# Post-norms of a two-model transformer kernel: the last squares summed on TensorE, copies and splits moved behind

## The reference

```
def rmsnorm(x, g):
    xf = x.astype(jnp.float32)
    y = xf * lax.rsqrt(jnp.mean(xf * xf, axis=-1, keepdims=True) + RMS_EPS)
    return (y * g.astype(jnp.float32)).astype(x.dtype)

    x = x + rmsnorm(merged @ w_out[l], norm_mix_post[l])
    h = rmsnorm(x, norm_mem_pre[l])
    ...
    x = x + rmsnorm(memory_cross_attention(h, mem_n, w_mq[l], w_mkv[l], w_mo[l]), norm_mem_post[l])
    h = rmsnorm(x, norm_ffn_pre[l])
    ...
    x = x + rmsnorm(y, norm_ffn_post[l])
```

## Time and profile before

| what | value |
|---|---|
| median of three runs | 3776.49 us |
| the three runs | 3774.99, 3776.49, 3776.53 us |
| the profiled execution | 3774.35 us |
| its span | 3772.5 us |
| TensorE busy (matmuls) | 3590.9 us, 95% of the span |
| VectorE busy | 2018.5 us, 54% |
| ScalarE busy | 1441.1 us, 38% |
| DMA | 333.13 MB, mean 88 GB/s |
| mean granted clock of TensorE | 0.991 |

### The profile page before, as it was taken

One profiled execution on the slowest core, in us unless ns is written; L12 is line 12 of the kernel. 1 busy time (PEld: TensorE's weight loads), 2 busy tenths in 40 slices (PEclk: granted clock), 3 DMA queues, 4 the chain that ended last, 5 costly groups with the idle time before them and its releaser, 6 DMA issues.

```text
span 3772.5 us, 52548 instructions
## 1 busy us (share of the span) xinstructions
PE 3590.9 (95%) x19348; PEld 2948.0 (78%) x19348; DVE 2018.5 (54%) x3396; ACT 1441.1 (38%) x2252; POOL 241.9 (6%) x384
## 2 busy tenths in 40 slices
PE   8999989999999999899999988999999998899998
PEld 6788877887787887688778776788888777677886
DVE  5634466777764355677774466443233444644345
ACT  3344344332324534533233366332122234743232
POOL 0000000001000000000000052000000002620000
PEclk9999999999999999999999999999999999999999
DMA  3222322445322233144551102111211112112222
GB/s 138 89 73 95 98 81 95 144 145 195 117 95 78 73 106 112 51 143 146 187 162 56 51 2 42 45 51 61 67 61 61 56 67 56 31 45 81 97 95 83
DMA packets 113070, 333.13 MB, mean 88 GB/s; under 512 B 32792, under 2 KB 33688, under 8 KB 112408
## 3 DMA queue, kind: packets, MB, share of 16 engines
q1 hardware_dynamic: 74112, 265.23, 21.3%
q0 software_dynamic: 14400, 52.44, 4.2%
q10 hardware_dynamic: 24408, 13.46, 1.6%
HBM read 328.99 MB, written 6.00 MB: 89 GB/s over the span
## 4 chain that ended last, share of the span: by engine, by line
PE 83%; DVE 7%; ACT 5%; issue 2%; DVEq 1%; POOL 0%; DMA 0%; ACTq 0%; POOLq 0%; SPq 0%
PE PS L602 14%; PE PS L603 14%; PE PS L604 13%; PE PS L984 11%; PE PS L987 11%; PE PS L985 10%; PE PS L677 1%; PE PS L1112 1%; PE PS L771 1%; ACT PB L1671 1%; ACT FULL_P L1671 1%; PE PS L783 1%; DVE HVAL L1946 1%; DVE Y L2359 1%; DVE MX L2385 1%
## 5 line engine op out<-in xcount | busy, mean ns | idle before, releaser
L1902 DVE TENSOR_TENSOR WL<-RAW,WH 128x1024 fp32r<-128x1024 f32 x494 | 604.6, 1224 | 572.9 <-ACT WH L1330 567.4
L1330 ACT ACTIVATE WH<-RAW 128x1024 fp32r<-128x1024 f32 x494 | 521.4, 1056 | 638.6 <-PE PS L987 350.3
L602 PE MATMUL PS<-HHI,WH 128*128 128x512 f32 x1632 | 648.5, 397 | 14.7 <-DVE HLO L1939 7.5
L603 PE MATMUL PS<-HLO,WH 128*128 128x512 f32 x1632 | 642.3, 394 | 0.0
L604 PE MATMUL PS<-HHI,WL 128*128 128x512 f32 x1632 | 636.7, 390 | 0.0
L984 PE MATMUL PS<-H2HI,WH 128*128 128x512 f32 (+1 forms) x1336 | 470.8, 352 | 0.0
L985 PE MATMUL PS<-H2LO,WH 128*128 128x512 f32 (+1 forms) x1336 | 445.0, 349 | 0.0
L987 PE MATMUL PS<-H2HI,WL 128*128 128x512 f32 (+1 forms) x1336 | 388.2, 351 | 0.0
L602 PEld LDWEIGHTS PS<-HHI,WH 128*128 128x128 f32 x1632 | 306.8, 188 | 100.1 <-DVE HLO L1939 15.5
L604 PEld LDWEIGHTS PS<-HHI,WL 128*128 128x128 f32 x1632 | 306.8, 188 | 68.1
L603 PEld LDWEIGHTS PS<-HLO,WH 128*128 128x128 f32 x1632 | 307.3, 188 | 61.1 <-issue 0.5
(11 more groups left out here) (340 smaller groups left out, 5650.3 us busy)
## 6 DMA issues: line engine op xcount, KB each, us to landing
RAW<-in_stream SPq DMA_DIRECT2D x494, 512.0 KB, 3.7
MODW<-in_modw POOLq DMA_DIRECT2D x96, 512.0 KB, 4.5
bias_rows<-in_rpb ACTq DMA_DIRECT2D x8, 476.2 KB, 6.1
X<-in_x SPq DMA_DIRECT2D x4, 512.0 KB, 5.5
MEM<-in_mem ACTq DMA_DIRECT2D x2, 1024.0 KB, 4.9
CROW<-in_crow POOLq DMA_DIRECT2D x4, 512.0 KB, 4.9
BIAS<-bias_rows ACTq DMA_DIRECT2D x8, 224.0 KB, 4.7
GRID<-bias_rows ACTq DMA_DIRECT2D x8, 224.0 KB, 4.8
```

What stands on the lines that cost most here:

```text
L602: nc.tensor.matmul(out, WH[:, slot, b * P:(b + 1) * P], hi, start=start, stop=False)
L603: nc.tensor.matmul(out, WH[:, slot, b * P:(b + 1) * P], lo, start=False, stop=False)
L1330: A(WH[:, d, :], RAW[:, s, :], ACT.Copy).then_inc(high_split, 1)
L1902: TT(WL[:, d, :], RAW[:, s, :], WH[:, d, :].bitcast(F32), ALU.subtract).then_inc(split_ready, 1)
```

## The change

- `statistics(n, direct, last_square)` waits only for the adds of the first `KB - direct` squares, sums `ACC` into the bank, issues the eight dummies, waits for each of the last `direct` squares itself, and adds it into the same bank with a matmul from `SQ`. `direct` is 1, and 2 behind `w_mo`. VectorE's `add_squares` leaves those squares out.
- ScalarE squares ahead of copying, and signals the square by `sq_ready`; behind `w_mo` two squares come before two copies.
- The `split_high` of the last evacuation goes behind `root`. VectorE's matching `split_low` goes behind `residual`, except at the first model's mixer output, where it stands between `root_inverse` and `residual`.
- The table preloads at the mixer output and at `w_down` go ahead of the squares.
- Behind `w_down` TensorE waits for all `modulation` steps before `statistics`.

The diff, cut to its core (the counting of marks and the second model's parts that repeat the pattern are left out):

```diff
-            def statistics(n):
-
-                keep_clock(8)
-                m.add("sqt", KB - 1)
-                pe.wait_ge(sq_taken, m.at("sqt"))
+            def summed_over(src, n, start, stop):
+
                 for c0 in range(0, n, T):
                     c1 = min(c0 + T, n)
-                    last = nc.tensor.matmul(FLAT[:, 6 * T + c0:6 * T + c1], ONES[:], ACC[:, c0:c1], start=True, stop=True)
+                    last = nc.tensor.matmul(FLAT[:, 6 * T + c0:6 * T + c1], ONES[:], src[:, c0:c1], start=start, stop=stop,
+                                            skip_group_check=True)
+                return last
+
+            def statistics(n, direct=1, last_square=None):
+
+                m.add("sqt", KB - 1 - direct)
+                pe.wait_ge(sq_taken, m.at("sqt"))
+                summed_over(ACC, n, True, False)
+                keep_clock(8)
+                if last_square is None:
+                    m.add("sq", KB - direct)
+                for j in range(direct, 0, -1):
+                    if last_square is None:
+                        m.add("sq")
+                        pe.wait_ge(sq_ready, m.at("sq"))
+                    else:
+                        pe.wait_ge(y_squared, last_square)
+                    last = summed_over(SQ[:, (KB - j) % 2, :], n, False, j == 1)
                 last.then_inc(stat_done, 1)
...
+                pe.wait_ge(mod_used, (l + 1) * MOD_LAYER)
                 statistics(T)
...
-                A(Y[:, k, :], bank(3 * p), ACT.Copy)
-                A(dst[:, 0:n], bank(3 * p), ACT.Square, scale=D ** -0.5).then_inc(taken[p], 1)
-                split_high()
+                A(dst[:, 0:n], bank(3 * p), ACT.Square, scale=D ** -0.5).then_inc(sq_ready, 1)
+                A(Y[:, k, :], bank(3 * p), ACT.Copy).then_inc(taken[p], 1)
+                if k < KB - 1:
+                    split_high()
...
+                act.preload_act_table_set("natural_log_exp_and_others")
                 squares(of_y, T)
-                act.preload_act_table_set("natural_log_exp_and_others")
                 root(T)
+                split_high()
...
-            def add_squares(k, n, arrived):
+            def add_squares(k, n, arrived, direct=1):
 
                 if k == 0:
                     return
+                if k >= KB - direct:
+                    arrived(k)
+                    return
...
                 def post(gain, next_gain, last=False):
                     root_inverse(T)
                     residual(gain, False)
+                    split_low()
...
                 for k in range(KB):
                     add_squares(k, T, y_arrived)
-                    split_low()
+                    if k < KB - 1:
+                        split_low()
                 root_inverse(T)
...
+                split_low()
                 residual(G_MIXP, True, between=split_two)
```

More of the change, by code:

```diff
@@ L899, in _ @@
                 statistics(T)
-                m.add("sq", KB)
                 m.add("max", 16)
@@ L946, in _ @@
                     unit_out(last)
-                m.add("sq", KB // 2)
-                statistics(T)
+                statistics(T, 2)
                 sum_squares(T)
@@ L1308, in _ @@
                     quarter_down()
-                statistics(TA if full else T)
+                statistics(TA if full else T, 1, (l + 1) * KB)
         @block.scalar
@@ L1343, in square_slot, with squares @@
                 return SQ[:, k % 2, :]
-            def squares(src, n, before=None):
+            def squares(src, n, before=None, direct=1):
                 for k in range(KB):
@@ L1573, in of_mo @@
                     p = (m.n["units"] - 1) % SLOTS
-                    A(Y[:, k, :], bank(3 * p + k % 2), ACT.Copy)
-                    sq = A(dst[:, 0:n], bank(3 * p + k % 2), ACT.Square, scale=D ** -0.5)
-                    sq.then_inc(taken[p] if k % 2 else sq_ready, 1)
+                    A(dst[:, 0:n], bank(3 * p + k % 2), ACT.Square, scale=D ** -0.5).then_inc(sq_ready, 1)
                     if k % 2:
-                        split_high()
-                squares(of_mo, T)
+                        A(Y[:, k - 1, :], bank(3 * p), ACT.Copy)
+                        A(Y[:, k, :], bank(3 * p + 1), ACT.Copy).then_inc(taken[p], 1)
+                        if k < KB - 1:
+                            split_high()
+                squares(of_mo, T, direct=2)
                 root(T)
+                split_high()
                 squares_summed(of_x, T)
@@ L1609, in of_down @@
                     m.add(f"use{k % 2}")
[L1610 to L1613, removed]
+                    A(dst[:, 0:n], bank(3 * (k % 2)), ACT.Square, scale=D ** -0.5).then_inc(sq_ready, 1)
+                    A(Y[:, k, :], bank(3 * (k % 2)), ACT.Copy).then_inc(taken[k % 2], 1)
                 if l == DEPTH - 1:
@@ L1844, in of_y2 @@
                     m.add(f"use{p}")
-                    A(Y2[:, k, 0:n], FLAT[:, 3 * p * T:3 * p * T + n], ACT.Copy)
-                    A(dst[:, 0:n], FLAT[:, 3 * p * T:3 * p * T + n], ACT.Square, scale=D ** -0.5).then_inc(taken[p], 1)
-                    split_high()
+                    A(dst[:, 0:n], FLAT[:, 3 * p * T:3 * p * T + n], ACT.Square, scale=D ** -0.5).then_inc(sq_ready, 1)
+                    A(Y2[:, k, 0:n], FLAT[:, 3 * p * T:3 * p * T + n], ACT.Copy).then_inc(taken[p], 1)
+                    if k < KB - 1:
+                        split_high()
                 n2 = TA if full else T
@@ L1882, in _ @@
                     A(dst[:, 0:n2], Y2[:, k, 0:n2], ACT.Square, scale=D ** -0.5).then_inc(y_squared, 1)
-                m.add("sqt", KB - 1)
+                m.add("sqt", KB - 2)
                 root(n2)
+                split_high()
         @block.vector
@@ L1926, in y_arrived @@
                     m.add(f"use{j % 2}")
-                for p in range(2) if k == 1 else (k % 2,):
-                    dve.wait_ge(taken[p], m.at(f"use{p}", 1))
+                if k < KB - 1:
+                    sq_arrived(k)
+                else:
+                    m.add("sq")
+                    dve.wait_ge(taken[k % 2], m.at(f"use{k % 2}", 1))
             def root_inverse(n):
@@ L2234, in mo_arrived @@
                 def mo_arrived(k):
-                    if k == 1:
-                        m.add("sq")
-                        dve.wait_ge(sq_ready, m.at("sq"))
                     if k % 2:
                         m.add(f"use{k // 2 % 2}")
-                        dve.wait_ge(taken[k // 2 % 2], m.at(f"use{k // 2 % 2}", 1))
+                    if k < KB - 2:
+                        sq_arrived(k)
                     else:
                         m.add("sq")
-                        dve.wait_ge(sq_ready, m.at("sq"))
+                    if k == KB - 1:
+                        dve.wait_ge(taken[1], m.at("use1", 1))
                 for k in range(KB):
-                    add_squares(k, T, mo_arrived)
-                    if k % 2:
+                    add_squares(k, T, mo_arrived, 2)
+                    if k % 2 and k < KB - 1:
                         split_low()
@@ L2364, in residual2 @@
                         last.then_inc(x_ready, 1)
+                m.add("sq", KB)
                 dve.drain()
```

## The result

The changed kernel is slower, close to what was forecast: 3796.01 us median of five runs (3791.88 to 3802.52) against 3776.49 before. The ratio is 1.0056, with a 95% interval from 1.0043 to 1.0069. The forecast was 3793.5. The profiled execution of the changed kernel took 3800.71 us (span 3798.9), 4.7 more than the median of its runs. The profiled execution of before lies 2.1 under its median. So of the 26.4 us between the two spans, 6.8 come from which executions were profiled.

What follows compares the result with a forecast made beforehand. TensorE, with 83% of the chain, was taken to bound the kernel, each norm's tail being an exposed chain. Terms 1.0 + 3.5 + 1.0 + 4.0 + 7.5 = 17.0 us on 3776.5 gave 3793.5, range 3786 to 3802.

Steps and rivals of the forecast that it cites:

- The path: In each norm's tail the logarithm waits for TensorE, whose eight dummies stand between two sums, however early the square is.
- The price of the relay: In each tail, from the start of ACC's sum to the logarithm: 3.91 us at 512 columns, 4.77 at 768.
- Where ACC is early: Logarithm later by +0.5 behind `w_mo` in each layer, +0.36 and +0.63 at the second model's mixer output.
- Where ACC is late: Logarithm later by +1.73 behind `w_down` per layer, +2.13 and +1.84 at second model's MLP outputs, +3.75 at K/V phase end.
- The moved split: First model's mixer output: split behind the root delays the residual +2.25, leaving 1.8 us at K/V phase end per layer.
- The clock: Rival, 15%: TensorE idles without dummies before the sums, clock falls, six stages lose up to 1.7 each: +10, giving 3803.5.
- The sum: Stage differences of 1.0, 3.5, 1.0, 4.0 and 7.5 make 17.0 us, put onto the median 3776.5: 3793.5.
- What costs nothing: Splits moved behind the root in other stages, the later RAW load and the moved table load: no cost.

## Why the prediction was right, and where its sizes were off

- *The path.* Right: in every tail of the changed kernel ScalarE waits for the square's sum with the square long done.
- *The price of the relay.* Forecast 3.91 us from ACC's sum to the logarithm, 4.77 at 768 columns. Measured at the full clock: 3.70 to 3.81, and 4.56 (2445.85 to 2450.41). Back to back, a sum holds TensorE 0.86, not the 0.96 that I had read behind an idle gap.
- *Where ACC is early.* Forecast +0.5 behind `w_mo`, +0.36 and +0.63 at the second mixer. The tails grew by 0.29, 0.15 and 0.42.
- *Where ACC is late.* Forecast +1.84 at the kernel's end: measured 1.74. Behind `w_down`, first layer, forecast +1.73: measured 1.84, with the relay 0.1 shorter and the modulation's end 0.2 later than reckoned. The same +1.73 was taken over for the second layer without its rows. There the tail of before was 4.47, not 5.03, and the change took it to 8.74, by 4.27, of which the clock is 1.6. The others have the fallen clock on top: 8.95 against 5.26 behind the first MLP, where 2.13 were forecast.
- *The moved split.* Forecast 1.8 a layer, measured 1.4 and 1.7 in the length of the K/V phase up to its last product.
- *The clock.* This is the term that was mis-sized. I gave it to a rival with 15% and 10 us. Four tails of the profiled execution had it. By their distances from ACC's sum to the logarithm (6.47, 5.46, 5.45, 6.34) less those at the full clock (3.81 three times, 4.56), it cost 2.7 + 1.6 + 1.6 + 1.8 = 7.7 us there. The first K/V tail lost more than the 1.7 a stage that the rival allowed. What I had held against the rival, that the first layer's K/V tail of before ran at the full clock, didn't bear on it: the dummies filled its gap, and the change took them from there.
- *The sum.* That 3793.5 came so near to the median of 3796.0 is in part luck. The profiles differ by 26.4: 13.0 in the tails without the clock, 7.7 for the clock in the tails, 3.1 in the K/V phases and 2.6 in the other stretches. The forecast's terms stand against 16.1 of that with 17.0, and the clock, which it put at nothing, makes the measured time longer by an amount that differs from execution to execution.
- *What costs nothing.* The other moved splits left no mark where the stretch behind them can be compared: from the first tail of the second model to its next it took 564.14 us before and 564.12 after, and from the last logarithm to the end of the span it is 14.89 us before (3757.61 to 3772.5) and 14.92 after (3783.98 to 3798.9), with VectorE's last split in between, beside the output. The table load did cost something at the first model's mixer output of before, which the prediction didn't say: it began at 470.86, took 1.28, and the logarithm followed at 472.15, 1.47 behind ACC's sum (470.68) instead of the 1.16 of `w_mo`. Moving it was worth 0.3 us there, and the relay took that and more.

## What to carry to other kernels

When a chain is shortened on two engines, look in the queue of the third for what stands ahead of its last step; filler that was free ahead of a wait is on the path behind it. Filler is placed where the engine would idle next and nowhere else: against none, eight dummies were worth 13 us ahead of one wait, and cost 21 between two sums and 19 behind that wait (3808.4 against 3789.1). The better filler is work that has to be done anyway, such as the early part of a sum right behind the products.

## What the runs showed of the hardware

In these traces a gap on TensorE behind dense products is often, and not always, followed by the level of 1.2 GHz in the very work that ends the gap: 3.62 us for dummies that take 1.95, 1.75 for a sum of 1.12. Counted over all tails of the twelve traces by TensorE's longest gap in each: of 13 with 3.4 us or more 11 had a granted clock of 0.5, of 35 with 1.9 to 3.4 us 17 had it, and of 11 with 1.5 to 1.9 us none. At the end of the K/V phase it fell behind both gaps of 4.25 us in the kernel before with its dummies behind the wait, and behind three of four gaps of 3.46 in the changed kernel and the one with the mixer's split ahead. Behind `w_down` in the changed kernel, 2.91 us led to it and 2.68 did not; with the dummies first, gaps of 2.58 and 2.89 at the same place did not. I can't say from these runs when it falls, only that longer gaps had it more often and that one profile of a kernel doesn't tell its price. The Trainium skill, page "TensorE: Matmul & The Clock Gate", section "HAM oscillation — how this bites in real kernels", warns that idle gaps between groups of matmuls throw the clock back. The traces agree in part, by the counts above: a gap made it likelier and not certain. The experiments give it a price here: 13 us for twelve tails without filler (3789.1 against 3775.9).
